# One piece of the first modulation chunk, the grouped decay functions, and the order around the output gate, in a two-block transformer kernel

## The reference

```python
# modulation: six chunks of 1024 columns from the silu of the condition
shift1, scale1, gate1, shift2, scale2, gate2 = split(silu(c) @ w_mod + b_mod, 6)
h = rms_norm(x, norm1_g) * (1 + scale1) + shift1
# Hyena filters
hid = sin(freq * (z @ w1 + b1)); hid = sin(freq * (hid @ w2 + b2))
filt = (hid @ w3).reshape(n, 2, 2, 512) * exp(-t_norm * abs(decay))
taps = concat([fwd, 0, flip(bwd[1:])])
taps = taps / (sum(abs(taps), axis=0) + EPS); filter = rfft(taps)
# gated linear attention (GLA), forward and backward, in chunks of 64 tokens
log_a = log_sigmoid(a_low @ w_a2 + b_a) / 16
cum = cumsum(log_a); q_dec = q * exp(cum); k_inv = k * exp(-cum)
k_to_end = k * exp(cum_last - cum); chunk_state = k_to_end.T @ v
y_gla = rms_norm(o, g) * silu(og)            # og: the output gate
# second block: local attention with dilated windows, and latent attention,
cq = rms_norm(h[..., o3:o4]); ckv = rms_norm(h[..., o4:o5])   # 384 and 256 wide
```

## Time and profile before

| | before |
|---|---|
| median of 3 runs | 1752.64 us (1748.89 to 1754.97) |
| the profiled execution, its own time | 1748.85 us |
| its span in the trace | 1746.9 us |
| TensorE busy / weight loads | 1639.6 us (94%) / 1398.5 us |
| VectorE / ScalarE / GpSimd busy | 1086.5 us (62%) / 868.3 us (50%) / 8.6 us |
| mean granted TensorE clock | 0.970 |
| weights and inputs read | 294.9 MB, 169 GB/s over the span |

### The profile page before, as it was taken

How to read it: one execution, slowest core, us unless ns; L and a number is a source line. 1 busy time by engine, 2 the same in 40 slices (tenths; PEclk the granted TensorE clock), 3 DMA queues, 4 the chain that set the end, 5 groups by cost and what they waited for, 6 DMA issues and landing times.

```text
span 1746.9 us, 23040 instructions
## 1 busy us (share of the span) xinstructions
PE 1639.6 (94%) x9780; PEld 1398.5 (80%) x9780; DVE 1086.5 (62%) x1316; ACT 868.3 (50%) x1021; POOL 8.6 (0%) x19
## 2 busy tenths in 40 slices
PE   6999999999999999999989988999998997899998
PEld 2787878699996777889888866799986975799986
DVE  5568463354575788985466556665566567665555
ACT  5555534734544777774343365454444346354433
POOL 0000000000000000000000000000000000000000
PEclk9899999899999899999989999999999998999999
DMA  6635312124754799996544322555553540555540
GB/s 230 225 97 198 106 71 74 49 97 127 238 171 160 282 335 350 366 370 236 180 150 156 124 73 73 177 179 197 170 193 121 169 145 25 169 174 188 169 169 24
DMA packets 132317, 297.43 MB, mean 170 GB/s; under 512 B 5207, under 2 KB 16776, under 8 KB 131256
## 3 DMA queue, kind: packets, MB, share of 16 engines
q1 hardware_dynamic: 130192, 287.93, 47.8%
q0 software_dynamic: 1120, 5.46, 1.0%
q10 hardware_dynamic: 904, 2.58, 0.4%
HBM read 294.90 MB, written 1.05 MB: 169 GB/s over the span
## 4 chain that ended last, share of the span: by engine, by line
PE 79%; DVE 11%; ACT 8%; issue 2%; DMA 0%; ACTq 0%; DVEq 0%
PE bank L439 78%; DVE cut L1421 3%; ACT cut L2377 2%; PE bank L452 1%; ACT arena L2577 1%; DVE stat L1635 1%; ACT pairs L2383 1%; DVE XT L2245 1%; DVE pairs L2252 0%; DVE XT L2239 0%; ACT arena L2586 0%; DVE stat L2225 0%; DMA arena<-in_posemb 0%; DVE arena L1442 0%; DVE XT L2222 0%
## 5 line engine op out<-in xcount | busy, mean ns | idle before, releaser
L1421 DVE TENSOR_TENSOR cut<-raw,cut 128x2048 fp32r<-128x2048 f32 (+1 forms) x268 | 606.0, 2276 | 391.6 <-ACT cut L2377 391.0
L439 PE MATMUL bank<-pairs,cut 128*128 128x256 f32 (+1 forms) x5480 | 692.2, 287 | 23.8 <-DVE cut L1421 8.8
L439 PEld LDWEIGHTS bank<-pairs,cut 128*128 128x128 f32 (+1 forms) x5480 | 679.6, 192 | 36.1 <-issue 17.6
L2377 ACT ACTIVATE cut<-raw 128x2048 fp32r<-128x2048 f32 (+1 forms) x268 | 506.1, 1899 | 337.7 <-PE bank L439 318.4
L439 PE MATMUL bank<-cut,pairs 128*128 128x512 f32 (+1 forms) x2460 | 585.9, 398 | 14.7 <-DVE cut L1421 9.0
L439 PEld LDWEIGHTS bank<-cut,pairs 128*128 128x128 f32 x2460 | 460.8, 191 | 128.4 <-DVE cut L1421 12.6
L439 PE MATMUL bank<-arena 128*128 128x128 f32 (+10 forms) x748 | 184.4, 405 | 25.2 <-DMA arena<-in_posemb 7.6
L439 PEld LDWEIGHTS bank<-arena 128*128 128x128 f32 (+4 forms) x748 | 109.7, 193 | 78.8 <-issue 54.5
L2383 ACT ACTIVATE pairs<-arena 128x256 fp32r<-128x256 f32 (+1 forms) x81 | 37.5, 496 | 80.3 <-DVE arena L2289 51.4
L1429 DVE TENSOR_TENSOR pairs<-arena,pairs 128x256 fp32r<-128x256 f32 (+1 forms) x81 | 40.1, 528 | 31.2 <-ACT pairs L2383 31.0
L452 PEld LDWEIGHTS bank<-cst,arena 128*128 128x128 f32 x264 | 32.8, 149 | 33.3 <-DVE arena L2340 11.9
(11 more groups left out here) (289 smaller groups left out, 882.1 us busy)
## 6 DMA issues: line engine op xcount, KB each, us to landing
raw<-in_moe_w_gate SPq DMA_DIRECT2D x32, 1024.0 KB, 7.2
raw<-in_moe_w_up SPq DMA_DIRECT2D x32, 1024.0 KB, 7.0
raw<-in_moe_w_down SPq DMA_DIRECT2D x32, 1024.0 KB, 6.8
raw<-in_w_in SPq DMA_DIRECT2D x30, 1024.0 KB, 5.2
raw<-in_w_mod SPq DMA_DIRECT2D x24, 1024.0 KB, 5.3
raw<-in_ffn_w_gate SPq DMA_DIRECT2D x22, 1024.0 KB, 5.1
raw<-in_ffn_w_up SPq DMA_DIRECT2D x22, 1024.0 KB, 5.1
raw<-in_ffn_w_down SPq DMA_DIRECT2D x22, 1024.0 KB, 5.0
```

The costliest lines, as they stand in the source:

```text
L439: return pe.matmul(o, l, r, start=start, stop=stop, skip_group_check=True)
L1421: v.tensor_tensor(both[:, PIECE:PIECE + n], M.raw[K.place(i)[0]][:, 0:n], both[:, 0:n].bitcast(F32), ALU.subtract).then_inc(*up("lo_w", i))
L2377: a.activation(M.cut[K.slot(i)][:, 0:n], M.raw[K.place(i)[0]][:, 0:n], ACT.Copy).then_inc(*up("hi_w", i))
```

## The change

It has five parts.

**The opening.** The first modulation chunk is not cut. `mod_whole(0, ...)`, until now used for later chunks and moved up in the file, takes its two pieces raw and multiplies in plain float32, four products from each; the first half stands ahead of the first four filter products, the second ahead of the other four. `mod_chunk(0)` is gone, and with it the cuts of its pieces. SyncE's queue starts with the condition `cc`, the constants and the first piece, then the decay table, then the further pieces; ScalarE's queue starts with the position table. Silu and the parts of the condition come after the first sine, and the loads of `dft`, `xT` and `vecs` are issued after that.

**The filter's second sums.** VectorE adds the four blocks of magnitudes into one (`magnitudes`) ahead of `cut_until(8)`, so that TensorE sums with 4 products instead of 16. On VectorE the scale factors now stand before `filter_sums(1)`.

**The decays.** Weights and bias are one array of 64 rows (`w2z`; bias in row 0, ones in the rows of GA beside it, memset by VectorE), so each block's z is one product on 64 rows. ScalarE takes the four absolute values and exponentials first and the four logarithms after, in four buffers `LW`; VectorE takes the four minima first.

**The output gate.** "og" becomes a `group` over banks 2 and 3 with a step after each quarter: 24 products, key decays, 24 products, states, 48 products.

**The latent sums.** While the local steps run, `ahead[0]` is 1. VectorE adds the squares of the latent columns after head 5 (three adds of 256 columns, `sqs`), so `latent_sums()` has 4 products instead of 10.

The diff, cut to its core:

```diff
+    def mod_whole(c, k0, n, b):
+        for k in range(k0, k0 + n):
+            if k % 4 == 0:
+                whole[0] = take(D["w_mod"], k, 4, 512 * c, 512, raw=True)
+            if k == 0:
+                claim(("modrow", c), ("mrow", c), (b,))
+            P.wait_ge(*at("sct"))
+            last = mm(bank[b][:, :], M.sct[:, 4 * k:4 * k + 128].bitcast(F32), whole[0].hi[:, k % 4, :], k == 0, k == 7)
...
+    mod_whole(0, 0, 4, 1)
     for o_ in range(2):
         for i in range(2):
+            if (o_, i) == (1, 0):
+                mod_whole(0, 4, 4, 1)
+                late.append(0)
...
-    mod_chunk(0)
     filter_spectrum(1)
...
-        P.wait_ge(*K.load("w2z", 2))
-        chain(o[:, :], [(M.GA[96:128, i * 128:i * 128 + 128], M.W2[96:128, :]),
-                        (C("ones")[96:97, :], M.W2B[96:97, :])]).then_inc(*up("la", i))
+        P.wait_ge(*at("GA1"))
+        P.wait_ge(*K.load("w2z"))
+        mm(o[:, :], M.GA[64:128, i * 128:i * 128 + 128], M.W2[64:128, :], True, True).then_inc(*up("la", i))
...
-    project("og", W, 2592, 4, (HL,), 8, lambda m: ("OG", m))
+    steps = [key_decays, states, lambda: None, lambda: None]
+    group("og", 0, W, 2592, 4, (HL,), 8, lambda m: ("OG", m), banks=(2, 3), each=lambda: steps.pop(0)())
...
+        P.wait_ge(*at("sqs"))
+        for c, X2 in enumerate((M.CSQ, M.CSK)):
             for i in range(2):
-                last = chain(o[:, 2 * c + i:2 * c + i + 1], [(X2[:, k, 128 * i:128 * i + 128], C("ones")[:, 0:1])
-                                                             for k in range(nk)])
+                last = mm(o[:, 2 * c + i:2 * c + i + 1], X2[:, 0, 128 * i:128 * i + 128], C("ones")[:, 0:1], True, True)
+    ahead[0] = 1
     local_step()
...
+    def magnitudes():
+        AB = M.AB[1]
+        w(*at("AB", 1))
+        v.tensor_tensor(AB[:, 0, :, :], AB[:, 0, :, :], AB[:, 1, :, :], ALU.add).then_inc(*up("v"))
+        w(*at("v"))
+        v.tensor_tensor(AB[:, 0, 0, :], AB[:, 0, 0, :], AB[:, 0, 1, :], ALU.add).then_inc(*up("ABs", 1))
     cut_until(5)
     filter_out(1)
+    magnitudes()
     cut_until(8)
...
-    filter_sums(1)
     w(*at("mod", 0))
     factors("x", M.mod[:, 8:16, 0], M.cols("scl0", 8), "norm1_g")
     factors("c", M.mod[:, 8:16, 1], M.cols("scl1", 8), "norm1_g")
+    filter_sums(1)
...
     for i in range(4):
-        lw = M.LW[i % 2]
+        lw = M.LW[i]
         w(*at("la", i))
-        if i >= 2:
-            w(*at("LA", i - 2))
         a.activation(lw, M.bank[K.bank("la", i)][:, :], ACT.Abs).then_inc(*up("LAe", i))
         w(*at("LAe", i))
         a.activation(lw, lw, ACT.Exp, scale=-1.0).then_inc(*up("a"))
-        w(*at("a"))
-        a.activation(lw, lw, ACT.Ln, bias=1.0).then_inc(*up("LAl", i))
+    w(*at("a"))
+    for i in range(4):
+        a.activation(M.LW[i], M.LW[i], ACT.Ln, bias=1.0).then_inc(*up("LAl", i))
...
+    sp.dma_start(M.cc, D["cc"]).then_inc(*up("ld_cc", by=16))
     sp.dma_start(M.cst[:, 0:early], D["consts"][:, 0:early]).then_inc(*up("ld_cst", by=16))
-    sp.dma_start(M.dcy, D["hy_decay"].partition_broadcast(128)).then_inc(*up("ld_dcy", by=16))
...
+        if i == 1:
+            sp.dma_start(M.dcy, D["hy_decay"].partition_broadcast(128)).then_inc(*up("ld_dcy", by=16))
```

More of the change, by code:

```diff
@@ L677, in filter_sums @@
         o = claim(("hsm", o_), ("hsum", o_), (2, 3, 4, 5, 6, 7))
-        P.wait_ge(*at("AB", o_))
+        P.wait_ge(*at(("AB", "ABs")[o_], o_))
         for c in range(4):
-            last = chain(o[:, c:c + 1], [(M.AB[o_][:, i, d, 128 * c:128 * c + 128], C("ones")[:, 0:1])
-                                         for i in range(2) for d in range(2)])
+            parts = [(0, 0)] if o_ else [(i, d) for i in range(2) for d in range(2)]
+            last = chain(o[:, c:c + 1], [(M.AB[o_][:, i, d, 128 * c:128 * c + 128], C("ones")[:, 0:1]) for i, d in parts])
         last.then_inc(*up("hsm", o_))
@@ L845, in tensor_program @@
         last.then_inc(*up("cum", d))
-    for i in range(4):
-        o = claim(("ke", i), ("KEe", i))
-        for d in range(2):
-            sides = [(C(("SG" if i < 2 else "SF") + "fb"[d]), M.LA[:, i, d * 256:d * 256 + 256])]
-            if (i, d) == (2, 0):
-                sides.append((C("ones"), M.LA[:, 3, 0:256]))
-            if (i, d) == (3, 1):
-                sides.append((C("ones"), M.LA[:, 2, 256:512]))
-            last = chain(o[:, d * 256:d * 256 + 256], sides)
-        last.then_inc(*up("ke", i))
@@ L874, in tensor_program, with key_decays @@
-    project("og", W, 2592, 4, (HL,), 8, lambda m: ("OG", m))
+    def key_decays():
+        for i in range(4):
+            o = claim(("ke", i), ("KEe", i))
+            for d in range(2):
+                sides = [(C(("SG" if i < 2 else "SF") + "fb"[d]), M.LA[:, i, d * 256:d * 256 + 256])]
+                if (i, d) == (2, 0):
+                    sides.append((C("ones"), M.LA[:, 3, 0:256]))
+                if (i, d) == (3, 1):
+                    sides.append((C("ones"), M.LA[:, 2, 256:512]))
+                last = chain(o[:, d * 256:d * 256 + 256], sides)
+            last.then_inc(*up("ke", i))
@@ new lines, in states @@
+    def states():
+        for d in range(2):
+            o = claim(("ss", d, 0), ("SS", d, 0))
+            P.wait_ge(*at("GV", 3))
+            P.wait_ge(*at("KE", 3))
+            for j in range(2):
+                last = chain(o[:, j * 256:j * 256 + 256],
+                             [(M.KE[:, 2 + i, d, j * 128:j * 128 + 128], M.GV[:, 2 + i, j * 256:j * 256 + 256])
+                              for i in range(2)])
+            last.then_inc(*up("ss", d, 0))
+        for n in range(3):
+            for d in range(2):
+                c = n if d == 0 else 3 - n
+                r = slice(64 * (c % 2), 64 * (c % 2) + 64)
+                o = claim(("ss", d, n + 1), ("SS", d, n + 1))
+                for j in range(2):
+                    last = mm(o[:, j * 256:j * 256 + 256], M.KE[r, c // 2, d, j * 128:j * 128 + 128],
+                              M.GV[r, c // 2, j * 256:j * 256 + 256], True, True)
+                last.then_inc(*up("ss", d, n + 1))
@@ L1318, in tensor_program @@
     local_step()
+    ahead[0] = AHEAD
     local_step()
@@ L1464, in vector_program @@
         v.tensor_scalar(a64, a64, PI_F, -PI_F, ALU.min, ALU.max).then_inc(*up("angc", layer))
-    cut_until(1)
+        if layer == 0:
+            condition()
     def taps(i, q):
@@ L1690, in vector_program @@
             query_turned(4 + 2 * (i - 5))
+    v.memset(M.GA[64:96, :], 1.0).then_inc(*up("GA1"))
     for i in range(4):
```

96 lines of the change are left out of this document (38 added, 58 removed).

## The result

The changed kernel takes 1726.66 us (median of 4 runs, 1724.55 to 1737.07), the kernel before 1750.77 us beside it (4 runs, 1747.87 to 1754.97). The ratio is 0.9872 with a 95% interval of 0.9826 to 0.9919: 1.3% shorter, clear of noise though under 2%. The ratio stands for 22.4 us, the two medians differ by 24.1. The forecast was 1726 us.

The account below looks back on a forecast made before the run. TensorE, busy 94% of the span, was taken as the bound. Gains of 12.7 (opening), 10.9 (decays) and 1.0 us (local attention) sum to 24.6, giving 1724.3 or 1728.0 us; forecast 1726, range 1714 to 1740 us.

Parts of the forecast that it names:

- The opening: 12.7 forecast: Up to the first input columns: 9.0 us from an earlier second spectrum plus 3.7 us from the scale factors coming first.
- the end of the second spectrum: Opening: the second filter spectrum ends at 50.3 us against 59.4, 9.0 us earlier.
- 0.9 us as a mean: Opening: clock loss added for the one-column sums, half of the 1.7 us lost by the chunk behind them before.
- The clock's rise: Opening: full-width products from 12.4 us raise TensorE's clock after 4.8 us, at 17.2 us.
- The rival of the late rise: Opening: the chunk's first half does not raise the clock; opening loses 4.7, gains 3.7 us; 1738 us total; chance 0.16.
- the late second piece: Opening: the chunk's second weight piece, met at 21.6 us, lands at 25, costing 3.4 us; 1729 us total; chance 0.08.
- The factors and second sums: 3.7 forecast: End of opening: factors ahead of the second sums gain 3.7 us; sums shrink to 8 records beside ScalarE's work.
- The decays: 10.9 forecast: Decays through output gate: shorter products, grouped functions and new order end the stage at 358.6 us instead of 369.5.
- against the rival: Decays: the clock falls, the four products and part of the projection at half speed, some 5 us; 1731 us; chance 0.13.
- the prediction's second estimate: Decays: by the skill's switch cost of some 2.66 us with drain, six table loads would be worth 16 us.
- The local attention: 1.0 us gained forecast: Second block's local attention: earlier copy and saved low clock against a wait for adds; between 3.5 gained and 2.5 lost.
- the prediction's own signs of being wrong: Opening ending after 80 us, decays' stage over 45 us, or a new wait of several microseconds behind 370 us.

Follow-up runs that it names:

- the loads alone: Changed kernel with the logarithm again behind each block's exponential, seven table loads instead of one: decays' stage 47.10 us, median 1741.8 us.
- the run with two products: Changed kernel with each block's z in the decays again a product on 32 rows and one on 1 row: decays' stage 43.59 us, median 1732.64 us.
- twelve variants: The twelve kernels of the experiments, the changed kernel with one or several parts undone or altered: medians from 1722.71 to 1741.8 us.

## Why the prediction was right, and where it was wrong

- **The opening: 12.7 forecast, 8.25 measured.** The step that failed is the end of the second spectrum, 50.3 us forecast and 54.6 measured. The product began at 13.53 us instead of 12.4 (it waited for the condition, whose silu follows the first sine; that sine waited for VectorE, which waited until 8.14 us for a small table). The three groups at full pace took 3.63 us each where 3.4 were set, 0.7 us in all, the sums 0.4 us more. The largest part, 2.1 us, is the clock behind the one-column sums: 0.9 us as a mean was taken, and the spectrum lost 2.9 us. The kernel with both sums shortened shows that this was the price of the sums themselves. Its size varies: in three of the ten traces with these sums in the changed opening it was 1.8 us, sums and spectrum together, in seven 3.4 to 3.5, and none of the ten was without it, as the mean of 0.9 allowed for.
- **The clock's rise** was right: 4.4 us after the first full-width product, 4.8 taken. That 64-row products do not raise it but keep it is shown from both sides: eight records in 7.16 us in front of any full-width product, 3.70 behind. The rival of the late rise did not come, nor that of the late second piece (no wait at 22.94 us).
- **The factors and second sums: 3.7 forecast, 3.5 measured,** 1.6 by the order and 1.9 by the shorter sums. The prediction gave all of it to the factors and called the shorter sums covered by ScalarE's work; the run with 16 products shows that they are not.
- **The decays: 10.9 forecast, 12.02 measured.** The keys came in time, with no wait where 0.6 us was left, and the 64-row products kept the clock, against the rival. Undone one at a time the parts cost 9.6, 6.1 and 2.5 us, 18.2 in sum and more than the whole. A likely reason is that the low clock of the two products and the loads cover each other, since in the trace of before TensorE has no wait between the decay products and the cumulative ones, and with the loads alone it has 4.7 us; no run undoes both parts. By the Trainium skill ("ScalarE: Activation LUTs", Table sets), where logarithm and exponential share a set, grouping would have saved nothing. Here a load of 1.28 us stood at each change between the two functions, and the six loads cost 9.6 us of stage, neither nothing nor the 16 us of the prediction's second estimate.
- **The local attention: 1.0 us gained forecast, 4.87 lost.** The step that failed is the first: that cuts moved behind the softmax bring the copy forward by 1.8 us. The copy hangs on head 4's exponential, and that on TensorE's own scores, which no cut delayed; the look-ahead left the wait at 2.90 us. The wait for the adds was forecast at about 3 us and was 4.57, because the shorter look-ahead put a cut of 1536 columns ahead of head 6's mask, and the adds stand behind both; with two pieces of look-ahead it was 3.46. By the prediction's own signs of being wrong, a new wait of several microseconds behind 370 us, this one counts against it, although a wait of about 3 us was forecast there. (The rows that the prediction names for the cut ahead of a late mask show the cut and no mask.)
- **The total was right by compensation.** The places gave 15.4 us of the 24.6 forecast; 8.9 us came from the remainder, which the prediction put at nothing: 6.2 us from a higher clock and 2.7 us from shorter waits. The clock part is luck of the profiled execution: the mean remainder of the changed kernel and its twelve variants is 1562.9 us, with 78.6 us at the low level, so the changed kernel's trace stands 6.9 us on the lucky side, and that of before, with 77.7 us at the low level, on neither. How much of this is in the medians too is open: the interval of the ratio, 0.9826 to 0.9919, reaches from 14 to 30 us, and holds both 15.4 and 24.

## What to carry to other kernels

A chain of short products, one column wide or on few rows, costs about as much again through the clock that it takes, its own or that of what follows (3.2 and 2.9 us for the first sums, 3.3 and 2.8 us for the decay products): let another engine add first, so that few are left, or put full-width work in front. Before you hand a reduction to a slower engine, look at what stands ahead of it there: four products behind a wait of 4.57 us were worse than ten without. And judge an edit by its own stage, aligned between traces: the decays repeated to 0.02 us, the local attention to 0.4 and the opening to 2, where the remainder moved by 12.

## What was not expected of the hardware

- Products on 32 rows and 1 row let the granted clock fall to 0.5 with TensorE never idle, 5.4 us after they began in the run with two products and 2.4 us after in the kernel before. Sixteen records of 64-row products in a row did not raise a low clock (16.8 to 30.7 us in the kernel before), and eight did not lower a high one (3.70 us).
- 32 one-column records took the clock of what stood behind them in all twelve traces that have them there (0.75 on the mean for the changed kernel's spectrum); 8 did not in the two that have 8 (1.00).
- The time of unchanged work differs from trace to trace by up to 12 us in 1563, and half of the time at the low clock level accounts for it to within 2 us.
